# RWKV's triangular inverse by doubling: levels 2 to 4 multiply 32 by 32 blocks, four products of 32 rows for a pair of heads

## The chip, the cores and the metric

One core of a Trainium2 chip runs the whole program. The metric is the device time of one execution in microseconds (us), the median of several executions.

## The reference, cut to what matters

The program computes two transformer-like blocks on 256 tokens of width 1024. The change is inside the second block's bidirectional RWKV-7 mixer (8 heads of 64, two directions):

```python
def _rwkv7_step(state, inp):
    r, w, k, v, kk, kka = inp
    sa = jnp.einsum('dbhvk,dbhk->dbhv', state, kk)
    state = state * w[..., None, :] - sa[..., :, None] * kka[..., None, :] + v[..., :, None] * k[..., None, :]
    y = jnp.einsum('dbhvk,dbhk->dbhv', state, r)
    return state, y
...
_, ys = lax.scan(_rwkv7_step, state0, xs)
```

The kernel does this scan in chunks of 64 tokens. Inside a chunk, `sa` of a token depends on the `sa` of the tokens before it, which is a triangular system of 64 by 64 for each head and direction. The kernel inverts that triangle by doubling: at level n the diagonal blocks of 2^n rows are already inverted, and two products make the inverse of the blocks of 2^(n+1) rows. There are five levels after the first, so that the whole 64 by 64 triangle is inverted after level 5. After level n the inverse is zero outside its diagonal blocks of 2^(n+1) rows, which at levels 1 to 4 are at most 32 rows.

## The kernel before, in words

All matrix products of the linear layers use weights in two parts (high and low). A ring of six weight tiles is filled by SyncE's DMAs (L490), ScalarE makes the high part (L2316), GpSimd the low part (L505), and TensorE multiplies three times (L529 to L531, or L597 to L599 for the products by token). The stage of the change lies between 848 and 945 us of the span, between the projection `qkv` and the output projection `out_2`.

In that stage, 16 cases (8 heads, 2 directions) are worked on for each of four chunks j = 0 to 3. The 16 cases are 8 "units" u of two heads: the first head of a unit is in partitions 0 to 63, the second in partitions 64 to 127. `heads` (L1098 to L1103, the matrix instruction is on L1101) issues two products of 64 by 64 by 64, one for each half of the partitions, and `per_unit` (L1105) calls it for the eight units, so that a call issues 16 products and fills one bank of PSUM, 128 partitions by 512 columns. Operands are f32, and the trace has two matmul records for each such product, so one call of `per_unit` is 32 records ("a product of a level" below means such a call). TensorE loads the left operand as weights and streams the right one past it.

The chunks are worked on in two pairs (two "lanes", j % 2). Per level and chunk the work is:

- `level_left(j, level)` on TensorE (L1147 to L1150): waits for `t_ev`, the transposed inverse of the level before, and multiplies `nt` by `tc` into the lane's bank 1. VectorE's `level_left` masks the result (L2128, called through L2164) into `uc`; the mask of a level is zero outside the blocks that this level joins.
- `level_both(j, level)` on TensorE (L1153 to L1161): waits for `u_ev` (the mask done) and for `tt_ev` (the copy of the level before), and multiplies `uc` by `ttc[j]` into the lane's bank 0. VectorE's `turned` transposes this in 32 by 32 blocks into `tc` (L2169, not after level 5), and ScalarE's `inverse` copies it into `ttc[j]` after that transposition (L2843).

Each engine works off its own list in the order written. For chunks 0 and 1 the TensorE order of a level is

```python
level_left(0, level)
level_left(1, level)
attention(4 + 2 * level)
level_both(0, level)
attention(5 + 2 * level)
level_both(1, level)
```

where `attention` interleaves one head of the dilated attention: an even step is `scores` (L1028) and `weighted_values` (L1048), an odd step is `turned_probabilities` (L1039, which waits for VectorE's L2085 and ScalarE's exponentials L2797). VectorE takes the scores out of PSUM (L2072), reduces them (L2075) and scales the weighted values (L2082, L2085) between its masks and its transpositions.

For chunks 2 and 3 a level is `level_left(2)`, `level_left(3)`, a piece of the chunk recurrence, `level_both(2)`, `level_both(3)`. The pieces are `from_state(0)` at level 1, `solve(0)` at level 2, `to_state(0)` at level 3, `from_state(1)` and `attention_by_feature` (L1075) at level 4 and `solve(1)` at level 5; all but the last-named function use products of 64 rows through `heads`. On VectorE, the norm of the attention (L2100, L2102) stands behind level 1's transpositions, the new state (L2180) and the outputs (L2188) ahead of level 3's transpositions, and the rest of the norm (L2107, L2110) behind them. After level 5, `half_row(0)` starts `out_2` when the last `tt_ev` has come. `first_products`, `second_products` and `third_product`, which make the inputs of the inversion, also use `per_unit`.

Of the kernel before, what the change touches and what calls it, by code (L numbers as in the profile page):

```python
# [44 lines left out]
RC = 64  # L45
# [594 lines left out]
def tensor_program(k, pe):  # L640
    s, mm, c = k.s, k.nc.tensor.matmul, Small(k)
# [29 lines left out]
    for b in range(KB):  # L671
        mm(ps, k.wdt_hi[:, b, :], op.hi[:, b, :], start=b == 0, stop=False)
        mm(ps, k.wdt_hi[:, b, :], op.lo[:, b, :], start=False, stop=False)
        last = mm(ps, k.wdt_lo[:, b, :], op.hi[:, b, :], start=False, stop=b == KB - 1)
# [148 lines left out]
    for i in range(2):  # L823
        for g in range(GROUPS):
            last = mm(k.bank[0][32 * g:32 * g + 32, 0:T], k.ones[:, 0:32], k.gn_sq[:, 2 * g + i, :], start=i == 0, stop=i == 1)
# [272 lines left out]
    def heads(bank, u, lhs, rhs, start=True, stop=True, shared=False):  # L1098

        for rows in (slice(0, HD), slice(HD, P)):  # L1100
            last = mm(bank[rows, u * RC:(u + 1) * RC], lhs[rows], rhs[rows], start=start, stop=stop,  # L1101
                      skip_group_check=shared)
        return last  # L1103

    def per_unit(bank, lhs, rhs):  # L1105

        for u in range(8):
            last = heads(bank, u, lhs(u), rhs(u))
        return last

    C_, B_, A_, Q_ = range(4)
    of = lambda x: lambda u: x[:, u, :]
    stack = lambda u: k.stack[:]
# [27 lines left out]
    def nth(j, level, levels):  # L1141

        return 2 * levels * (j // 2) + 2 * (level - 1) + j % 2 + 1

    def level_left(j, level):

        pe.wait_ge(s["t_ev"], nth(j, level, 5))  # L1147
        if level == 1:
            pe.wait_ge(s["qc_ev"], j + 1)
        per_unit(k.lane[j % 2][1], of(k.nt[j % 2]), of(k.tc[j % 2])).then_inc(s["u_mm"], 1)  # L1150

    def level_both(j, level):

        pe.wait_ge(s["u_ev"], nth(j, level, 5))
        if level == 1:
            pe.wait_ge(s["tt_first"], j + 1)
            pe.wait_ge(s["ac_ev"], j + 1)
            pe.wait_ge(s["bt_ev"], min(j + 1, NRC - 1))
        else:
            pe.wait_ge(s["tt_ev"], nth(j, level - 1, 5))  # L1160
        per_unit(k.lane[j % 2][0], of(k.uc[j % 2]), of(k.ttc[j])).then_inc(s["tt_mm"], 1)  # L1161

    def from_state(j):

# [53 lines left out]
    for level in range(1, 6):  # L1218
# [6 lines that stand above are left out]
# [35 lines left out]
    for level in range(1, 6):  # L1260
        level_left(2, level)
        level_left(3, level)
        if level == 1:
            from_state(0)
        elif level == 2:
            solve(0)
        elif level == 3:
            to_state(0)
        elif level == 4:
            from_state(1)  # L1270
            attention_by_feature()
        else:
            solve(1)
        level_both(2, level)
        level_both(3, level)
# [1666 lines left out]
def build_program(nc, a, out):  # L2942
    with ExitStack() as ctx:
        k = allocate(nc, ctx)
        block = ctx.enter_context(nc.Block())

        @block.sync
        def _(sp):
            sync_program(k, sp, a, out)

        @block.gpsimd
        def _(pool):
            gpsimd_program(k, pool)

        @block.scalar
        def _(act):
            scalar_program(k, act, a)

        @block.vector
        def _(v):  # L2960
            vector_program(k, v)

        @block.tensor
        def _(pe):
            tensor_program(k, pe)
# [84 lines left out]
```

## Time and profile before

| | us |
|---|---|
| median of 3 executions | 1185.81 (1185.35 to 1187.62) |
| the profiled execution, its own time | 1187.46 |
| its span, first to last instruction | 1185.7 |
| TensorE busy | 1154.6 (97%) |
| TensorE weight loads busy | 1079.5 (91%) |
| GpSimd busy | 900.6 (76%) |
| ScalarE busy | 623.7 (53%) |
| VectorE busy | 551.2 (46%) |

Some 1.8 us of the profiled execution lie outside its span. A busy TensorE means that some product is in flight; products overlap in it, so its busy share says that it is rarely empty, and not how full it is.

### The profile page before, as it was taken

How to read it: one execution, taken by the hardware profiler on the slowest of the kernel's cores; microseconds unless marked ns; L12 is line 12 of the kernel's file. 1: busy time of each engine (PE TensorE's matmuls, PEld its weight loads, DVE VectorE, ACT ScalarE, POOL GpSimd, SP SyncE). 2: the span in 40 equal slices, each digit the busy share in tenths (PEclk: the TensorE clock that was granted, in tenths of full speed). 3: DMA queues.
4: the chain of work that ended last, by engine and by line, in shares of the span. 5: the costliest groups of instructions: out<-in, count | busy, mean ns of one | idle time of the engine just before them, and what ended most of it. 6: DMA issues, size and time to landing. Idle time of an engine off the chain costs nothing.

```text
span 1185.7 us, 25232 instructions
## 1 busy us (share of the span) xinstructions
PE 1154.6 (97%) x10632; PEld 1079.5 (91%) x10632; DVE 551.2 (46%) x973; ACT 623.7 (53%) x1001; POOL 900.6 (76%) x689
## 2 busy tenths in 40 slices
PE   6999999999999999999999999999999999999998
PEld 6998999999997899998999999899989988999997
DVE  2553485543662122224644233757876555323334
ACT  5665676447635454444744444689342316444443
POOL 5987677876986999996899998599700015999994
PEclk9999999999999999999999999999999999999999
DMA  7655445655576666665566656556400034666663
GB/s 252 192 180 166 137 125 160 211 158 154 186 218 196 178 190 185 192 183 175 160 187 186 190 184 187 203 161 188 126 3 3 4 109 142 181 191 182 192 181 106
DMA packets 53776, 192.75 MB, mean 163 GB/s; under 512 B 6305, under 2 KB 7329, under 8 KB 53281
## 3 DMA queue, kind: packets, MB, share of 16 engines
q1 hardware_dynamic: 50640, 183.00, 51.1%
q10 hardware_dynamic: 3024, 8.16, 2.0%
q8 instruction: 84, 1.38, 0.5%
q14 instruction: 28, 0.22, 0.1%
HBM read 189.03 MB, written 1.05 MB: 160 GB/s over the span
## 4 chain that ended last, share of the span: by engine, by line
PE 90%; DVE 5%; ACT 2%; DMA 2%; issue 1%; POOL 0%; SPq 0%; DVEq 0%; ACTq 0%
PE product L529 18%; PE product L531 18%; PE product L530 18%; PE bank L597 7%; PE bank L599 7%; PE bank L598 7%; PE bank L1101 3%; PE product L1101 3%; PE product L695 1%; PE product L697 1%; PE product L696 1%; PE product L1048 1%; PE bank L529 1%; PE product L1028 1%; PE bank L530 1%
## 5 line engine op out<-in xcount | busy, mean ns | idle before, releaser
L505 POOL TENSOR_TENSOR weight_lo<-raw_ring,weight_hi 128x512 fp32r<-128x512 f32 x684 | 895.7, 1342 | 267.2 <-ACT weight_hi L2316 246.3
L2316 ACT ACTIVATE weight_hi<-raw_ring 128x1024 fp32r<-128x1024 f32 x338 | 357.0, 1060 | 406.0 <-DMA raw_ring<-in_ffn_gu 107.7
L529 PE MATMUL product<-operand_B_hi,weight_hi 128*128 128x256 f32 x1104 | 311.5, 282 | 1.7 <-POOL weight_lo L505 1.6
L530 PE MATMUL product<-operand_B_lo,weight_hi 128*128 128x256 f32 x1104 | 311.1, 282 | 0.0
L531 PE MATMUL product<-operand_B_hi,weight_lo 128*128 128x256 f32 x1104 | 310.9, 282 | 0.0
L529 PE MATMUL product<-operand_A_hi,weight_hi 128*128 128x256 f32 x776 | 223.7, 288 | 11.3 <-DVE weight_lo L1429 11.3
L531 PE MATMUL product<-operand_A_hi,weight_lo 128*128 128x256 f32 x776 | 219.8, 283 | 0.0
L530 PE MATMUL product<-operand_A_lo,weight_hi 128*128 128x256 f32 x776 | 219.6, 283 | 0.0
L529 PEld LDWEIGHTS product<-operand_B_hi,weight_hi 128*128 128x128 f32 x1104 | 208.0, 188 | 4.9 <-POOL weight_lo L505 2.1
L530 PEld LDWEIGHTS product<-operand_B_lo,weight_hi 128*128 128x128 f32 x1104 | 207.7, 188 | 3.0
L531 PEld LDWEIGHTS product<-operand_B_hi,weight_lo 128*128 128x128 f32 x1104 | 207.8, 188 | 0.0
L529 PEld LDWEIGHTS product<-operand_A_hi,weight_hi 128*128 128x128 f32 x776 | 147.3, 190 | 14.2 <-issue 13.6
L530 PEld LDWEIGHTS product<-operand_A_lo,weight_hi 128*128 128x128 f32 x776 | 146.9, 189 | 0.6 <-issue 0.2
L531 PEld LDWEIGHTS product<-operand_A_hi,weight_lo 128*128 128x128 f32 x776 | 147.0, 189 | 0.0
L597 PE MATMUL bank<-weight_hi,operand_B_hi 128*128 128x512 f32 x304 | 120.1, 395 | 2.5 <-DVE operand_B_lo L1761 2.5
L599 PE MATMUL bank<-weight_lo,operand_B_hi 128*128 128x512 f32 x304 | 119.8, 394 | 0.0
L598 PE MATMUL bank<-weight_hi,operand_B_lo 128*128 128x512 f32 x304 | 119.4, 393 | 0.0
L1761 DVE TENSOR_TENSOR operand_B_lo<-arena,operand_B_hi 128x256 fp32r<-128x256 f32 x76 | 76.3, 1005 | 81.7 <-ACT operand_B_hi L2633 81.7
L1852 DVE TENSOR_TENSOR pre<-product,rs 128x256 f32<-128x256 f32 x84 | 35.1, 418 | 127.3 <-PE product L531 127.3
L1771 DVE TENSOR_TENSOR arena<-product,pre 128x256 f32<-128x256 f32 x30 | 12.7, 425 | 127.7 <-ACT pre L2652 127.7
L597 PEld LDWEIGHTS bank<-weight_hi,operand_B_hi 128*128 128x128 f32 x304 | 57.1, 188 | 13.8 <-issue 2.5
L599 PEld LDWEIGHTS bank<-weight_lo,operand_B_hi 128*128 128x128 f32 x304 | 57.1, 188 | 13.3
(379 smaller groups left out, 1441.0 us busy)
## 6 DMA issues: line engine op xcount, KB each, us to landing
raw_ring<-in_w_in SPq DMA_DIRECT2D x99, 512.0 KB, 3.7
raw_ring<-in_ffn_gu SPq DMA_DIRECT2D x88, 512.0 KB, 3.6
raw_ring<-in_ffn_down SPq DMA_DIRECT2D x44, 512.0 KB, 3.6
raw_ring<-in_w_mlp_up SPq DMA_DIRECT2D x32, 512.0 KB, 4.2
raw_ring<-in_w_mlp_down SPq DMA_DIRECT2D x32, 512.0 KB, 4.2
raw_ring<-in_w_out SPq DMA_DIRECT2D x16, 512.0 KB, 4.2
raw_ring<-in_w_gmlp_v SPq DMA_DIRECT2D x8, 512.0 KB, 4.2
raw_ring<-in_w_branch_c SPq DMA_DIRECT2D x8, 512.0 KB, 3.5
```

What stands on the lines that cost most here:

```text
L505: last = k.nc.gpsimd.tensor_tensor(k.wlo[:, slot, part], k.raw[:, slot, part], k.whi[:, slot, part].bitcast(F32), ALU.subtract)
L529: mm(ps, w_hi, op.hi[:, b, :], start=b == 0, stop=False)
L530: mm(ps, w_hi, op.lo[:, b, :], start=False, stop=False)
L531: return mm(ps, w_lo, op.hi[:, b, :], start=False, stop=b == blocks - 1)
L597: mm(ps, hi, k.whi[:, slot, cols], start=j == 0, stop=False)
L598: mm(ps, lo, k.whi[:, slot, cols], start=False, stop=False)
L599: last = mm(ps, hi, k.wlo[:, slot, cols], start=False, stop=j == n - 1)
L1101: last = mm(bank[rows, u * RC:(u + 1) * RC], lhs[rows], rhs[rows], start=start, stop=stop, skip_group_check=shared)
L1761: nv.tensor_tensor(op.lo[:, j % KB, :], k.hid[:, j % KB, :], op.hi[:, j % KB, :].bitcast(F32), ALU.subtract).then_inc(s["op_ready"], 1)
L1771: nv.tensor_tensor(k.hid[:, j % KB, :], k.product[n][:, 0:T], k.pre[:, j % RING, :], ALU.mult).then_inc(s["evacuated"], 1)
L1852: nv.tensor_tensor(k.pre[:, ring, :], k.product[n][:, 0:T], k.rs[:], ALU.mult).then_inc(s["evacuated"], 1)
L2316: k.nc.scalar.activation(k.whi[:, slot, 0:w], k.raw[:, slot, 0:w], ACT.Copy).then_inc(k.s["hi_ready"], 1)
```

## The change

In levels 2, 3 and 4, `level_left` and `level_both` call a new function in place of `per_unit`. For each of the eight units it issues four products of 32 by 32 by 32 in place of two of 64 by 64 by 64: the two diagonal blocks of each of the two heads. Block q takes rows 32q to 32q + 31 of both operands and writes the same partitions of the bank. What lies outside the diagonal blocks in a bank keeps what the product of level 1 has left there. Levels 1 and 5, and every other user of `per_unit`, stay as they are.

```diff
+    def per_half_unit(bank, lhs, rhs):
+
+        for u in range(8):
+            for q in range(4):
+                rows, cols = slice(32 * q, 32 * q + 32), slice(32 * (q % 2), 32 * (q % 2) + 32)
+                last = mm(bank[rows, u * RC + 32 * (q % 2):u * RC + 32 * (q % 2) + 32], lhs(u)[rows, cols],
+                          rhs(u)[rows, cols], start=True, stop=True)
+        return last
+
+    by_level = lambda level: per_half_unit if 2 <= level <= 4 else per_unit
+
...
     def level_left(j, level):
...
-        per_unit(k.lane[j % 2][1], of(k.nt[j % 2]), of(k.tc[j % 2])).then_inc(s["u_mm"], 1)
+        by_level(level)(k.lane[j % 2][1], of(k.nt[j % 2]), of(k.tc[j % 2])).then_inc(s["u_mm"], 1)
...
     def level_both(j, level):
...
-        per_unit(k.lane[j % 2][0], of(k.uc[j % 2]), of(k.ttc[j])).then_inc(s["tt_mm"], 1)
+        by_level(level)(k.lane[j % 2][0], of(k.uc[j % 2]), of(k.ttc[j])).then_inc(s["tt_mm"], 1)
```

## Rows read from the trace of the kernel before

**Rows 1.** The page: TensorE's line, the granted clock, the chain that ended last.

```profile
PE 1154.6 (97%) x10632; PEld 1079.5 (91%) x10632; DVE 551.2 (46%) x973; ACT 623.7 (53%) x1001; POOL 900.6 (76%) x689
...
PEclk9999999999999999999999999999999999999999
...
PE 90%; DVE 5%; ACT 2%; DMA 2%; issue 1%; POOL 0%; SPq 0%; DVEq 0%; ACTq 0%
```

**Rows 2.** Busy time by stretch: stretch, length, busy and count by engine, clock, DMA.

```profile
873.70:880.50 6.80, 6.80 (x148) 6.02 (x145) 4.56 (x8) 2.78 (x7) 0.00 (x0) 1.00 0.01 2
...
922.10:928.70 6.60, 6.60 (x222) 6.58 (x224) 4.00 (x6) 2.79 (x4) 0.00 (x0) 1.00 0.01 2
```

**Rows 3.** Groups by form, TensorE: weights rows*columns, moving rows x columns, busy, mean ns.

```profile
L1101 PE MATMUL bank<-arena 64*64 64x64 f32 x1280 | 42.3, 220 | 0.9 <-DVE arena L2128 0.9
...
L1048 PE MATMUL product<-arena 128*128 128x64 f32 x64 | 8.8, 281 | 0.8 <-ACT arena L2806 0.8
...
L1007 PE MATMUL bank<-arena,block_ones 128*128 128x256 f32 x8 | 1.9, 379 | 0.0
...
L825 PE MATMUL bank<-arena,ones 128*32 128x256 f32 x16 | 1.1, 385 | 0.0
```

**Rows 4.** Timeline, one level of chunks 0 and 1: start, duration, engine, line.

```profile
866.94 1.10 PE L1101 MATMUL product<-arena 64*64 64x64 f32 x32
...
867.97 1.13 PE L1028 MATMUL product<-arena 64*128 64x256 f32 x4
...
869.03 1.10 PE L1048 MATMUL product<-arena 128*128 128x64 f32 x8
869.14 0.69 DVE L2072 SCALAR_TENSOR_TENSOR arena<-product,arena 128x512 f32<-128x512 f32 x1 [0.36 <-PE product L1028]
...
870.07 1.15 PE L1101 MATMUL bank<-arena 64*64 64x64 f32 x32
...
870.73 0.29 DVE L2085 TENSOR_TENSOR arena<-product,small 128x128 f32<-128x128 f32 x1
...
871.17 0.63 PE L1039 MATMUL product<-ident,arena 128*128 128x128 f32 x4
...
871.73 2.08 PE L1101 MATMUL bank<-arena 64*64 64x64 f32 x64
...
872.93 0.72 DVE L2169 STREAM_TRANSPOSE arena<-bank 128x512 f32<-128x512 f32 x1 [0.95 <-PE bank L1101]
...
873.70 1.15 PE L1101 MATMUL product<-arena 64*64 64x64 f32 x32
```

**Rows 5.** Timeline, levels 2 to 5 of chunks 2 and 3, same columns.

```profile
921.95 0.68 DVE L2128 TENSOR_TENSOR arena<-product,arena 128x512 f32<-128x512 f32 x1
922.09 3.11 PE L1101 MATMUL bank<-arena 64*64 64x64 f32 x96 [0.88 <-DVE arena L2128]
...
924.22 0.72 DVE L2169 STREAM_TRANSPOSE arena<-bank 128x512 f32<-128x512 f32 x1 [0.22 <-PE bank L1101]
...
925.04 3.90 PE L1101 MATMUL product<-arena 64*64 64x64 f32 x128
...
928.77 3.07 PE L1101 MATMUL bank<-arena 64*64 64x64 f32 x96
...
928.99 0.69 DVE L2188 COPY pre<-product 128x512 f32<-128x512 f32 x1 [0.24 <-PE product L1101]
...
931.67 4.83 PE L1101 MATMUL product<-arena 64*64 64x64 f32 x160
...
937.46 3.12 PE L1101 MATMUL bank<-arena 64*64 64x64 f32 x96
940.41 2.03 PE L1101 MATMUL product<-arena 64*64 64x64 f32 x64
```

**Rows 6.** Waits in 840 to 980 us: waiter, releaser, total us, times, longest.

```profile
POOL weight_lo L505 <- ACT weight_hi L2316: 109.8, 4, 84.8
...
PEld bank L1101 <- issue: 2.0, 11, 0.3
```

## The prediction

> **What bounds the kernel now.** I read the page first. TensorE is busy 97% of the span, the chain that ended last is 90% TensorE, and the granted clock is full in every slice [rows 1]. The change touches only the inversion of the triangles, so its stage decides. [...] In a level of chunks 0 and 1 a second chain runs beside TensorE's own and is as long as it: left product of lane 1 (866.94), scores (867.97), VectorE's L2072 (869.14) to L2085 (870.73), turned probabilities (871.17), `level_both(1)` (871.73), its transposition (872.93), next left product of lane 1 (873.70) [rows 4]. The links are 1.03 + 1.17 + 1.59 + 0.44 + 0.56 + 1.20 + 0.77 = 6.76 us. This chain holds only two of the level's four products. In chunks 2 and 3 TensorE waits 0.88 us for VectorE's masks ahead of level 2's `level_both(2)`, and the next left products start right behind VectorE's transpositions: 924.22 + 0.72 = 924.94, then 925.04 [rows 5].
>
> **The size of one product.** 24 calls change (3 levels, 4 chunks, 2 products). One takes 0.93 us: the 128 records from 925.04 to 928.77 are four calls, 3.73 / 4 [rows 5]. That is 16 rounds of 58 ns, each round the two halves of the partitions at once: single records last 220 ns, yet 1280 of them cover 42.3 us, 33 ns each [rows 3].
> What would a round of 32 by 32 cost? Eight records of 256 moving columns cover 1.9 us and one alone is 0.379, so a further one takes (1.9 - 0.379) / 7 = 217 ns, 0.85 ns a column [rows 3]; 64 columns are 54 ns of the 58, and 4 are fixed. Weight columns cost about as much: L1048 streams only 64 columns past 128 weight columns, and its 8 records take 1.10 us, (1.10 - 0.28) / 7 = 117 ns each [rows 3, 4]. With 32 of both I take 27 + 5 = 32 ns a round.
> How many blocks share a round? The new call has 64 records. That four narrow tiles of the array run at once is shown by L825, whose weights are 32 columns wide: 16 records of 256 columns cover 1.1 us, where one after another they would need 15 x 217 + 385 ns = 3.6 us, and four at once 3 x 217 + 385 = 1.04 [rows 3]. There the four differ by columns of the array, here by rows and columns; no row shows four groups of rows, but two groups do overlap. So 64 / 4 = 16 rounds x 32 ns = 0.51 us a call, 0.42 saved. Bounds: 16 x 27 = 0.43 us if nothing is fixed; two at once gives 32 x 32 ns = 1.02; one at a time gives 64 x 32 ns = 2.05. I take 0.51, since both the overlap of halves and the four narrow tiles are in rows.
>
> [...] The bank is one and the same for all four groups of rows, and already now two groups write one bank and run at 58 ns a pair, not 116 [rows 3, 5]. [...]
>
> **Where the saving lies on the path, chunks 0 and 1.** TensorE's own chain has four changed products in a level, 6.80 - 4 x 0.42 = 5.1 us; the other has two, 6.76 - 2 x 0.42 = 5.9 us, and takes over. So only `level_left(1)` and `level_both(1)` count: 2 x 3 levels x 0.42 = 2.5 us. What is late next is VectorE's scores work. The left and both products of chunk 0 cost and give nothing: they lie under L2072 to L2085 and under lane 1's transposition; without that cover they would give another 2.5. Level 5's `level_left(0)` becomes just as late as lane 1's transposition, and it comes right behind a change of tile size. A change of tile size costs 0.10 us from the left product to the scores (866.94 to 867.97 is 1.03, less 0.93) and 0.17 from `level_both(0)` to the transpositions (870.07 to 871.17 is 1.10, less 0.93; a part of it is the wait for L2085) [rows 4]; I take 0.13. One such is on the path: 2.4 us stay.
>
> **Chunks 2 and 3.** Here I follow the lists with the same lags: VectorE starts 0.24 us after a product's last record starts, TensorE 0.06 after VectorE's end, last record 0.48 after the first.
> Level 2: both left products are hidden, as the masks end at 921.95 + 0.68 = 922.63 whatever TensorE does (VectorE is at the attention's norm before them). `level_both(2)` stays at 922.09, `level_both(3)` starts at 922.69 behind its mask, its transposition runs 923.56 to 924.28, and level 3's `level_left(3)` starts at 924.34, not 925.04, and ends 924.85: 1.12 ahead of 925.97.
> Level 3: `to_state(0)` (96 records) is unchanged, less one change of tile size ahead of it and one behind (0.13 each): `level_both(2)` starts at 927.91, not 928.77. VectorE's output copy L2188, 0.69 us, waits for `to_state`'s end and now holds the transpositions back until 928.71; they end at 930.18. Level 4's `level_left(3)` starts at 930.24, not 931.67, and ends 1.85 us ahead.
> Level 4: another 0.13 ahead of `from_state(1)`, so `level_both(2)` is 1.72 us ahead (935.74, not 937.46). The two transpositions end at 937.18 and 937.93, level 5's `level_left(2)` runs 937.24 to 938.17, and `level_left(3)` starts at 938.17, not 940.41. That is 2.24 us ahead, 2.2. Level 5 is unchanged, TensorE works it off without a gap, and `half_row(0)` comes earlier by as much.
>
> **What comes behind.** All of `out_2` and `ffn2` moves up if the weights are there. GpSimd waits 84.8 us in one piece [rows 6] with the ring full, so the first tiles are ready, and the later loads are released by TensorE's own progress: they move with it. I cost this at nothing; if `ffn2` were limited by an absolute time of a DMA, the gain would shrink, but no DMA is in flight in this stage (share 0.01 [rows 2]). The new call has twice the instructions, 128 in place of 64 with the weight loads, on TensorE's list alone; no other engine's list, wait or DMA changes.
>
> Sum: 2.4 + 2.2 = 4.6 us. The profiled execution (span 1185.7, time 1187.46) would take 1182.9; it lies 1.65 above the median of the runs, 1185.81, and against that the forecast is **1181.2 us**. About 0.2%, 2.4 us, is what a measurement of this kernel can tell from no change.
>
> **Rivals.**
> *Two at once (slower).* The four groups of rows do not all overlap, only pairs. For it: nothing in the trace shows four groups of rows. Against: L825's four tiles. A call takes 1.02 us, 0.09 more. TensorE's chain then decides in chunks 0 and 1: 12 x 0.09 + 2 x 0.13 = 1.35 us. In chunks 2 and 3, level 2's left products hide in the 0.88 us gap: 10 x 0.09 + 5 x 0.13 = 1.55. Sum 2.9, **1188.7 us**. The point from which it turns slower is a call of about 0.86 us (54 ns a round of four), where what is saved on the path no longer pays for the changes of tile size. Chance 0.10.
> *One at a time (much slower).* [...] Against it are the pairs in [rows 5]. A call takes 2.05 us, 1.12 more: 12 x 1.12 + 0.3 in chunks 0 and 1, 12 x 1.12 - 0.9 + 0.7 in the others, 27 us, **1213 us**. Chance 0.05. [...]
> *Issue shows up.* A call of 0.93 us hides how TensorE's sequencer takes waits and instructions; one of 0.51 with twice the instructions hides less. The weight loads of L1101 waited for issue 11 times, 2.0 us, 0.18 each [rows 6]. If each changed call on the path (6 and some 8) lost that, 14 x 0.18 = 2.5 us, the gain is 2.1: **1183.7 us**. Against it: most of these waits are at changes of tile size, already counted. Chance 0.15.
> *It does not do what it says.* If all of it were hidden by VectorE, the time would stay at 1185.8; the rows give no cover for lane 1. Chance 0.02.
>
> [...]
>
> **How the numbers follow.** The forecast has a chance of 0.68. Its own range is from 0.43 us a call and free changes of size (6 x 0.50 = 3.0, and 2.24 x 0.50 / 0.42 + 0.4 = 3.1, sum 6.1, 1179.7 us) to about 1182.6 at 0.65 us a call (0.28 / 0.42 x 4.6 = 3.1). The range that should hold 8 in 10 takes in the issue rival and no change, and stops short of the two slow rivals: 1179.6 to 1187.0. Faster by over 0.2% (below 1183.4) takes the forecast and a quarter of the issue rival: 0.72. Within 0.2%: the rest of that rival, no change, and part of the pairs: 0.15. Slower (above 1188.2): 0.13.
>
> **What the changed profile would show.** L1101's neighbour, the new line, has 24 x 64 = 1536 records of 32*32 32x32. A group of 64 of them should last about 0.5 to 0.6 us from first to last start; 1.0 means pairs, 2.0 one at a time. The levels 2 to 4 of chunks 0 and 1 should repeat every 5.9 us, TensorE waiting there for VectorE (L2085 or L2169), where it waited for next to nothing. In chunks 2 and 3 the gap ahead of level 2's masks should grow from 0.9 to about 1.7 us. The stretch behind, from level 5's `level_left(3)` to the end, should keep its length (1185.7 - 940.4 = 245.3 us) within a few tenths. A period of 5.9 with a longer stretch behind would mean that the gain is given back to the weights; a lower granted clock in this stage would be a price that I have not counted.

## The result, and the profile after

| | before | after |
|---|---|---|
| median, us | 1186.50 (4 executions, 1185.35 to 1187.62) | 1201.68 (4 executions, 1197.29 to 1205.73) |
| profiled execution: time, span, us | 1187.46, 1185.7 | 1197.29, 1195.5 |
| mean granted clock of its span | 0.997 | 0.989 |

The ratio is 1.0123, 95% interval 1.0092 to 1.0154: slower by 15 us, where 4.6 us less was forecast. The profiled execution is the fastest of the four. Its page, answering to [rows 1], with the queue that carries the instructions:

```profile
span 1195.5 us, 26768 instructions
...
PE 1155.6 (97%) x11400; PEld 1078.5 (90%) x11400; DVE 548.5 (46%) x973; ACT 623.8 (52%) x1001; POOL 900.2 (75%) x689
...
PEclk9999999999999999999999999999989899999999
...
q8 instruction: 90, 1.47, 0.5%
```

There are 768 more matmul records and as many more weight loads, 1536 instructions, and the clock is no longer full in two of the slices. The queue of instructions moved 90 packets, 1.47 MB: 16 KB each. L1116 is the new products' line, and every line behind it stands 11 further down than before (L2096 was L2085, L2139 was L2128, L2180 was L2169). The timeline of TensorE in the changed levels (start, duration, engine, line, count, idle time before):

```profile
874.59 1.16 PE L1116 MATMUL bank<-arena 32*32 32x32 f32 x110
876.65 0.34 PE L1116 MATMUL bank<-arena 32*32 32x32 f32 x17 [0.89 <-issue]
...
881.26 0.99 PE L1116 MATMUL bank<-arena 32*32 32x32 f32 x92
884.11 0.47 PE L1116 MATMUL bank<-arena 32*32 32x32 f32 x35 [1.86 <-issue]
...
885.27 2.07 PE L1028 MATMUL product<-arena 64*128 64x256 f32 x4
...
895.50 1.13 PE L1028 MATMUL product<-arena 64*128 64x256 f32 x4
...
924.78 2.06 PE L1116 MATMUL bank<-arena 32*32 32x32 f32 x128 [1.64 <-issue]
928.35 0.26 PE L1116 MATMUL bank<-arena 32*32 32x32 f32 x1 [1.51 <-issue]
...
929.39 4.45 PE L1101 MATMUL product<-arena 64*64 64x64 f32 x96
...
939.66 5.37 PE L1101 MATMUL product<-arena 64*64 64x64 f32 x128
...
945.98 1.35 PE L1116 MATMUL bank<-arena 32*32 32x32 f32 x128
```

The two calls at 945.98 take 1.35 us, the last record's 0.2 included: about 0.58 us a call, so the four groups of rows do overlap, as forecast. But TensorE stops in the middle of calls, inside one and the same product form, and waits for nothing that the trace shows. Between the stops at 924.78 and 928.35 lie 128 matmul records and, as each has its own load, 256 instructions. And the four `scores` records at 885.27 take 2.07 us, where they took 1.13 in [rows 4]: the clock is halved (0.52 over 885.2 to 895.5). The waits for issue from 840 to 980 us (waiter, releaser, total, times, longest) and the busy time by stretch (length, busy time and count of PE, PEld, DVE, ACT, POOL, then granted clock, DMA share, GB/s) say how much of each:

```profile
PE bank L1116 <- issue: 6.8, 5, 1.9
PE product L1116 <- issue: 2.5, 2, 1.7
```

```profile
869.20:875.60 6.40, 5.92 (x324) 5.00 (x318) 4.64 (x9) 3.10 (x8) 0.00 (x0) 1.00 0.02 5
875.60:882.30 6.70, 5.45 (x269) 4.48 (x259) 4.41 (x9) 2.81 (x8) 0.00 (x0) 1.00 0.02 5
882.30:885.20 2.90, 1.09 (x100) 1.09 (x99) 1.01 (x2) 0.66 (x2) 0.00 (x0) 0.93 0.00 0
885.20:895.50 10.30, 10.30 (x218) 8.76 (x210) 4.71 (x9) 2.77 (x7) 0.00 (x0) 0.52 0.02 5
...
925.00:935.00 10.00, 8.20 (x382) 7.71 (x381) 4.59 (x7) 2.79 (x4) 0.00 (x0) 0.66 0.02 5
935.00:945.00 10.00, 7.36 (x291) 7.01 (x291) 3.66 (x6) 1.79 (x3) 0.00 (x0) 0.83 0.02 5
```

So there are two costs: seven stops for issue, 9.3 us, against none in `before` at this line, and a granted clock of 0.5 for most of 885 to 895 us and parts of 925 to 935 and of 935 to 945. By the trace's clock record these are 884.8 to 895.1, 925.8 to 932.6 and 939.4 to 942.8, 20.5 us in all. The first row also shows 642 instructions in 6.40 us without a stop: 10.0 ns each, so for two or three blocks TensorE went faster than it did for long (14.6 ns each in the burst below).

Since the work ahead of the stage varies by some us from one execution to the next, I compare the stage by itself: from the start of level 1's first transposition (L2169 in `before`) to the first L597 of `out_2` (first the two lines of `before`, then those of the change):

```profile
871.26 0.72 DVE L2169 STREAM_TRANSPOSE arena<-bank 128x512 f32<-128x512 f32 x1 [0.24 <-PE bank L1101]
...
945.01 0.50 PE L597 MATMUL bank<-weight_hi,operand_A_hi 128*128 128x512 f32 x1 [0.70 <-ACT arena L2843]
```

```profile
867.72 0.72 DVE L2180 STREAM_TRANSPOSE arena<-bank 128x512 f32<-128x512 f32 x1 [0.24 <-PE bank L1101]
...
953.28 0.50 PE L597 MATMUL bank<-weight_hi,operand_A_hi 128*128 128x512 f32 x1 [0.70 <-ACT arena L2854]
```

It took 945.01 - 871.26 = 73.7 us before and 953.28 - 867.72 = 85.6 us after, 11.8 more. Behind it the span is 240.7 us before and 242.2 after.

### The profile page after: what moved, and what is told of

It is laid out like the page before. It is cut to its first block, busy times and chain, and to the rows that moved or that the text cites. A ratio compares the mean times of both kernels' runs of the same rounds, so it can differ in the third digit from the quotient of the medians.

```text
span 1195.5 us, 26768 instructions
## 1 busy us (share of the span) xinstructions
PE 1155.6 (97%) x11400; PEld 1078.5 (90%) x11400; DVE 548.5 (46%) x973; ACT 623.8 (52%) x1001; POOL 900.2 (75%) x689
## 3 DMA queue, kind: packets, MB, share of 16 engines
q8 instruction: 90, 1.47, 0.5%
## 4 chain that ended last, share of the span: by engine, by line
PE 90%; DVE 4%; ACT 2%; DMA 2%; issue 2%; POOL 0%; DVEq 0%; ACTq 0%
PE product L529 18%; PE product L530 18%; PE product L531 18%; PE bank L597 7%; PE bank L599 7%; PE bank L598 7%; PE product L1101 3%; PE bank L1101 2%; PE product L1028 1%; PE bank L1116 1%; DMA raw_ring<-in_w_in 1%; PE product L695 1%; PE product L697 1%; PE product L696 1%; PE bank L529 1%
## 5 line engine op out<-in xcount | busy, mean ns | idle before, releaser
L597 PE MATMUL bank<-weight_hi,operand_B_hi 128*128 128x512 f32 x304 | 120.1, 395 | 2.5 <-DVE operand_B_lo L1772 2.5
L1772 DVE TENSOR_TENSOR operand_B_lo<-arena,operand_B_hi 128x256 fp32r<-128x256 f32 x76 | 79.3, 1044 | 87.3 <-ACT operand_B_hi L2644 87.3
L597 PEld LDWEIGHTS bank<-weight_hi,operand_B_hi 128*128 128x128 f32 x304 | 57.2, 188 | 13.7 <-issue 2.5
```

Source lines behind the costliest of these rows:

```text
L597: mm(ps, hi, k.whi[:, slot, cols], start=j == 0, stop=False)
L1772: nv.tensor_tensor(op.lo[:, j % KB, :], k.hid[:, j % KB, :], op.hi[:, j % KB, :].bitcast(F32), ALU.subtract).then_inc(s["op_ready"], 1)
```

## The experiments

The first theory (F) is that TensorE runs out of instructions; the rivals are that the 32-row form or its change of tile size stops TensorE, whatever the count (T), and a clock that the 32-row form itself lowers (C). Later C2 joins them: the clock falls because TensorE stands still for a part of the time. Ratios are against `before` on the same chip. Stage, issue waits and the time at clock 0.5 inside the stage are those of the one profiled execution. The last column is the median over the executions of the mean granted clock of a span (`before`, on the chips of the experiments: 0.997 to 0.999).

| run | ratio, 95% interval | stage, us | issue waits in it, us | clock 0.5 in it, us | clock |
|---|---|---|---|---|---|
| before | 1 | 73.7 | 0 | 0 | 0.997 |
| the change | 1.0123, 1.0092 to 1.0154 | 85.6 | 9.3 | 20.5 | 0.988 |
| chunk 1 alone | 0.9983, 0.9971 to 0.9994 | 72.0 | 0 | 0 | 0.998 |
| the same again | 0.9988, 0.9976 to 1.0 | 71.8 | 0 | 0 | 0.998 |
| half blocks | 1.0013, 1.0 to 1.0027 | 75.0 | 0 | 17.1 | 0.988 |
| burst | one execution, 1217.34 us | 104.9 | 14.7 | 27.3 | 0.986 |
| chunks 0 and 1 | 1.0023, 1.0005 to 1.0041 | 75.4 | 2.0 | 6.8 | 0.994 |
| chunks 2 and 3 | 1.007, 1.0046 to 1.0094 | 83.1 | 8.2 | 10.2 | 0.993 |
| 64-row twice | 1.021, 1.0176 to 1.0244 | 94.5 | 0 | 0 | 0.996 |
| chunk 0 alone | 1.0002, 0.9985 to 1.0019 | 73.7 | 0 | 0 | 0.997 |
| chunks 1 and 3 | 1.0019, 1.0003 to 1.0036 | 75.2 | 2.3 | 0 | 0.997 |
| half blocks in 1 and 3 | 0.9977, 0.9958 to 0.9996 | 71.1 | 0 | 0 | 0.998 |
| half blocks, filled | 1.0032, 1.0012 to 1.0051 | 72.3 | below 0.2 | 3.4 | 0.993 |
| half the units | 0.9953, 0.9935 to 0.9971 | 68.0 | 0 | 0 | 0.998 |

### A burst of the new form

```diff
     def level_both(j, level):
...
+        if (j, level) == (3, 4):
+            for n in range(16):
+                per_half_unit(k.lane[1][0], of(k.uc[1]), of(k.ttc[3]))
         per_unit(k.lane[j % 2][0], of(k.uc[j % 2]), of(k.ttc[j])).then_inc(s["tt_mm"], 1)
```

> The kernel before with level 4's second product of chunk 3 preceded by 16 calls of the 32-row form (same operands, same bank), 2048 instructions more in one stretch without any change of tile size or any wait. F: the stretch takes about 2048 / 256 x 3.5 = 28 us, with a gap after each 256 instructions, and the clock is halved in it. T: the stretch takes 16 x 0.55 = 9 us with no gap inside, as nothing changes size there. C: 16 x 0.55 us at full clock, 18 us if the clock is halved, no gaps.

The timeline of TensorE in the burst, and two of its stretches, then the queues' packets from 938.1 to 964.3 us (GB/s in 40 slices):

```profile
938.03 1.29 PE L1116 MATMUL bank<-arena 32*32 32x32 f32 x128 [1.13 <-issue]
941.77 1.68 PE L1116 MATMUL bank<-arena 32*32 32x32 f32 x128 [2.46 <-issue]
945.79 1.93 PE L1116 MATMUL bank<-arena 32*32 32x32 f32 x128 [2.34 <-issue]
...
964.25 0.42 PE L1116 MATMUL bank<-arena 32*32 32x32 f32 x12 [1.82 <-issue]
```

```profile
938.00:941.70 3.70, 1.29 (x128) 1.18 (x128) 0.00 (x0) 0.00 (x0) 0.00 (x0) 1.00 0.02 4
...
949.50:953.50 4.00, 1.93 (x128) 1.79 (x128) 0.00 (x0) 0.00 (x0) 0.00 (x0) 0.50 0.01 4
```

```profile
GB/s 0 0 25 0 0 0 0 0 25 0 0 0 0 0 25 0 0 0 0 25 0 0 0 0 0 25 0 0 0 0 25 0 0 0 0 25 0 0 0 0
...
q8 instruction: 7, 0.11, 1.6%
```

This is the disputed cost by itself. Nothing changes size here, nothing waits for another engine, and TensorE still stops after each 128 records and 128 loads. From 938.03 to 964.25 seven blocks of 256 instructions go by in 26.2 us, 3.75 us each, of which the work is 1.1 us at full clock ((1.29 - 0.19), the last record's own time left out). The pace is about the same with the clock full (3.74, the first) and halved (3.47 to 4.02), so it is not TensorE's array that sets it. All 16 calls took 28.9 us (935.71 to 964.60): F gave 28, T 9, and C 18 without gaps. T falls, and C alone does.

The instruction queue moves one packet of 16 KB a block: seven in this stretch for seven blocks. The packets' own records show that each takes 0.9 to 1.1 us and ends 1.2 to 1.6 us before TensorE starts again, at either clock (the first one in the view starts at 939.47, and TensorE starts at 941.77). So the stops keep step with the arrival of instructions. The blocks of 256 of theory F agree with the trace, and in this stream of small matmuls their arrival is not hidden: of the 3.75 us of a block, 1.5 to 2.5 are a wait for issue.

### The same count of instructions in the old form

```diff
+    def twice(bank, lhs, rhs):
+        per_unit(bank, lhs, rhs)
+        return per_unit(bank, lhs, rhs)
+
+    by_level = lambda level: twice if 2 <= level <= 4 else per_unit
```

> The kernel before with each of the 24 calls of levels 2 to 4 issued twice in the 64-row form: as many instructions as in the changed kernel, at 14.6 ns each. F: no issue wait over 0.5 us, full clock, since the blocks arrive about as fast as they are used (3.5 us against 3.7); time up by the work alone, 24 x 0.93 less the slack = 21 us, 1207. If the number of instructions in itself cost something (another wait for each, a pause per block), the time is above that, with gaps.

Its stage took 94.5 us, 20.8 more for 21 expected. The median of its two executions, 1211.31 us, is 24.1 above the kernel before on that chip; some 3 us of this lie outside the stage, and no run explains them. These are all of TensorE's waits from 866 to 970 us (L2858 is L2843 of before, L2100 is L2085):

```profile
PE bank L597 <- ACT arena L2858: 0.7, 1, 0.7
PE product L1039 <- DVE arena L2100: 0.2, 1, 0.2
```

As many instructions as in the change, and no wait for issue: 256 of them last 3.7 us in this form (14.6 ns each), which is the pace of the blocks in the burst (3.75 us). The number brought no wait by itself; it is the number per time.

### Only some of the chunks

The condition `2 <= level <= 4` gets an addition: `and j == 1`, `and j < 2`, `and j >= 2`, `and j == 0`, `and j % 2`.

> Only chunk 1's six calls (levels 2 to 4) use the 32-row products. Theory F (TensorE's instructions arrive in blocks of 256, one block in some 3.5 us at best, and the stalls are TensorE running out of them): a level of chunks 0 and 1 then holds about 430 instructions, 5.9 us at that pace, just what VectorE's chain allows. No issue wait over 0.5 us, full clock, period 5.9 us, time about 2.4 us below before: 1184. Rival T (it is the 32-row tile form, or the change between tile sizes, that stalls TensorE, whatever the count): with more changes of size per product than in the full change, stalls of 1 to 2 us as in the changed kernel and a time above before, about 1189. Rival C (the halved clock comes from 32-row products themselves): clock halved in this stage, no gain.

> The run on chunk 1 alone once more, for its ratio and for a second trace: 0.9975 to 0.999 of before, levels of chunks 0 and 1 of 6.0 to 6.3 us, full clock in them, no issue wait over 0.5 us.

The second trace of chunk 1 alone, one level:

```profile
875.88 1.15 PE L1101 MATMUL bank<-arena 64*64 64x64 f32 x32
876.98 0.64 PE L1039 MATMUL product<-ident,arena 128*128 128x128 f32 x4
877.54 0.75 PE L1116 MATMUL bank<-arena 32*32 32x32 f32 x64
878.23 1.15 PE L1101 MATMUL bank<-arena 64*64 64x64 f32 x32
879.31 0.75 PE L1116 MATMUL product<-arena 32*32 32x32 f32 x64
879.99 1.13 PE L1028 MATMUL product<-arena 64*128 64x256 f32 x4
...
882.08 1.15 PE L1101 MATMUL bank<-arena 64*64 64x64 f32 x32
```

A level takes 882.08 - 875.88 = 6.20 us, not 6.80, without any wait for issue. TensorE's own chain binds: a call with its change of size takes 0.68 (879.31 to 879.99), not 0.51. The level was expected at 5.9 us in the first of the two runs. With six calls this gains 1.8 and 1.9 us in the stage, 2.4 expected. It is the one version here that computes everything and came out below both kernels, by 0.12 and 0.17%; the upper end of the second interval is 1.0, so the gain is at the edge of what can be told.

> The 32-row form in all twelve calls of chunks 0 and 1, chunks 2 and 3 as before. A level of chunks 0 and 1 has about 560 instructions. F: 7.6 us a level at the fetch pace in place of 6.8, so some 2 to 4 us lost there with stalls of 1 to 2 us, and another few if the clock is halved; nothing lost in chunks 2 and 3: 1188 to 1191 us. T: about half of the full change's loss, 1194.

> The 32-row form in all twelve calls of chunks 2 and 3, chunks 0 and 1 as before. F: this stretch ran at about 450 instructions in 6.6 us before, which is already near the pace of one block of 256 in 3.5 us; with 12 x 64 more, three blocks, it loses about 3 x 3.5 = 10 us less what the calls save and less slack: 5 to 9 us over before, 1192 to 1196 us, most of the full change's loss. T: about half of it, as in the run on chunks 0 and 1.

The waits for issue, first of chunks 0 and 1, then of chunks 2 and 3:

```profile
PE bank L1101 <- issue: 1.1, 1, 1.1
PE bank L1116 <- issue: 0.9, 1, 0.9
```

```profile
PE bank L1116 <- issue: 4.4, 3, 2.1
PE product L1116 <- issue: 3.0, 2, 2.0
PE product L1101 <- issue: 0.8, 1, 0.8
```

Twelve calls each, and 2.0 against 8.2 us of stops, a loss of 0.2% against 0.7%. Some of each loss is the clock, which stood at 0.5 for 6.8 and 10.2 us of the stage. F said so from the counts: chunks 2 and 3 had 222 + 224 instructions in 6.60 us before [rows 2], 3.8 us a block, and no room for more; a level of chunks 0 and 1 had 148 + 145 in 6.80. T does not tell them apart.

> Only chunk 0's six calls use the 32-row form: as many calls as in the run on chunk 1 alone. By the chain of waits of the prediction nothing is on the path here: levels stay at 6.8 us, no issue wait over 0.5 us, the time is that of before, 0.999 to 1.002 of it. TensorE gets short idle pieces instead (some 0.8 us a level). Theory C2 (the clock falls after stretches in which TensorE is idle for a tenth of the time, whether for instructions or for VectorE, and not because of the 32-row form): the clock may fall here, and a level that it hits takes 8 us or more. If the clock depended on the form alone, this run and the one on chunk 1 would be alike (full clock).

Every level took 6.8 us, the stage 73.7, the ratio is 1.0002: the six calls of chunk 0 are hidden, as the prediction's second chain had it. The clock stayed full, though TensorE was busy only 6.32 us of 6.80:

```profile
871.80:878.60 6.80, 6.32 (x209) 5.36 (x208) 4.43 (x9) 2.78 (x7) 0.00 (x0) 1.00 0.01 2
```

> The 32-row form in chunks 1 and 3 (twelve calls). F: chunks 0 and 1 as in the run on chunk 1 alone, about 1.8 us gained. In chunks 2 and 3, 384 instructions more are one and a half blocks, 5 us at 3.6 us a block, against some 2 us saved and little slack: 2 to 4 us lost, with one or two issue waits of 1 us. Sum 0 to 2 us above before, 1187 to 1189. If the stalls did not come from the instructions, chunk 3 would gain another 1 to 2 us like chunk 1: 1183.

Chunks 0 and 1 gained 2.0 us (second to eighth transposition 18.45 us, before 20.41). Chunks 2 and 3 lost 3.0 from their first to their last transposition (25.2 for 22.2) and 0.3 behind it, with 2.3 us of waits for issue. This is what F expected of the stage; the whole came out at 1189.16 us, just above its 1187 to 1189.

### Half of the work, to take the instructions away

```diff
-            for q in range(4):
+            for q in (0, 2):
```

> The changed kernel with only blocks q = 0 and 2 of each unit: half of the inverse of levels 2 to 4 is left out. All 24 calls use the 32-row form, with 64 instructions a call as before the change. F: hardly any issue wait, clock full, 1181 to 1184 us. T and C: stalls and halved clock as in the changed kernel, 1195 us or more.

Here half of the inverse of levels 2 to 4 is left out. F alone was wrong, and so was its time: 1188.88 us, for 1181 to 1184. No stop for issue is left, as F said and T did not, but the clock is halved all the same (timeline and stretch):

```profile
886.61 2.07 PE L1028 MATMUL product<-arena 64*128 64x256 f32 x4
```

```profile
881.90:895.60 13.70, 13.47 (x244) 11.46 (x239) 6.55 (x14) 5.57 (x14) 0.00 (x0) 0.50 0.01 2
```

Ahead of the fall TensorE was busy 5.30 of 5.90 us. Was it the idle time, then, or the form? Three runs were made for that.

> As the run before, but with blocks q = 0 and 2 alone in chunks 1 and 3 (half of the inverse of their levels 2 to 4 is left out), so no more instructions than before the change, and chunks 0 and 2 in the 64-row form that keeps TensorE busy. C2: clock full in chunks 0 and 1 (it was halved for 13.7 us with half blocks in all chunks), levels of 5.9 to 6.2 us there, and with no block of instructions added a further 1 to 2 us gained in chunks 2 and 3: 1182.5 to 1184. If the 32-row form with half of the array unused lowers the clock, it falls here too and the gain is gone.

("The run before" is the one on chunks 1 and 3.) Full clock, the stage 2.6 us shorter than before, of which chunks 0 and 1 give 2.3. The time is 1184.5 us, for 1182.5 to 1184. With the form in every second chunk alone the clock stays.

The next run adds to the half blocks one 64-row product of chunk 0 a level (`if j == 0 and 2 <= level <= 4: per_unit(...)` ahead of `level_left`).

> The half-block run (q = 0 and 2 in all chunks, half of the inverse of levels 2 to 4 left out), and ahead of chunk 0's first product of levels 2 to 4 the 64-row product once more, into the same bank: 0.93 us of extra work a level, laid where TensorE was idle. C2 (the clock fell because TensorE stood still for a tenth of the time): TensorE is busy 98% or more of these levels, the clock stays full, levels take about 6.2 us, and first to eighth transposition 18.5 to 19 us, where the half-block run without the extra work took 21.4: more work, less time. If the form lowers the clock, it is halved here as well and the levels take 7 us or more.

This one settles nothing. The profiled execution had the full clock in the levels of chunks 0 and 1 and shorter ones than without the extra work (19.9 us against 21.4 from second to eighth transposition). But TensorE was busy only 6.09 of 6.50 us, not 98%, the clock was halved for 3.4 us in chunks 2 and 3, and in the other executions it was 0.989 to 0.994.

```profile
875.50:882.00 6.50, 6.09 (x182) 5.24 (x177) 4.29 (x9) 2.77 (x7) 0.00 (x0) 1.00 0.02 5
```

So the idle time was given to the old form:

```diff
+    def half_the_units(bank, lhs, rhs):
+        for u in range(4):
+            last = heads(bank, u, lhs(u), rhs(u))
+        return last
+
+    by_level = lambda level: half_the_units if 2 <= level <= 4 else per_unit
```

> The kernel before with only units 0 to 3 in the 24 calls of levels 2 to 4 (half of the inverse of those levels is left out): 64-row form, 0.47 us a call and half the instructions, so TensorE stands still about as much as with half blocks in all chunks, without the 32-row form and without more instructions. If standing still is enough to lower the clock, mean clock 0.988 to 0.993 over the executions, halved for 7 to 14 us somewhere in these levels, time near before. If it is the 32-row form (fewer rows of the array at work in each product), the clock stays at 0.997, levels of chunks 0 and 1 take 5.9 us, and the time is 4 to 5 us below before.

Here, too, half of the inverse of those levels is left out. L2185 is L2169 of before.

```profile
877.95 0.68 PE L1101 MATMUL product<-arena 64*64 64x64 f32 x16 [0.35 <-DVE arena L2185]
878.56 1.13 PE L1028 MATMUL product<-arena 64*128 64x256 f32 x4
...
883.81 0.68 PE L1101 MATMUL product<-arena 64*64 64x64 f32 x16 [0.35 <-DVE arena L2185]
```

```profile
877.00:883.00 6.00, 5.23 (x93) 4.29 (x88) 4.34 (x8) 2.91 (x9) 0.00 (x0) 1.00 0.01 3
```

TensorE is busy 5.23 of 6.00 us, less than with half blocks, at clock 1.00; the six executions had 0.996 to 1.0. The time is 0.9953 of before, the stage 5.7 us shorter. So standing still alone is not what halves the clock here, nor is the number of instructions, which half blocks left as before. What the runs with a halved clock in the stage have in common, against all others, is 32-row products in both lanes (or the burst); that is a pattern over fourteen traces, and what in the form does it was not tested. Single falls of 3.4 us stand outside the stage too, where nothing was changed (861.5 to 864.9 in the second run of chunk 1 alone). With stage lengths of 68.0 and 75.0 us, the two runs with half of the work differ by 7.0 us, for some 17 us at clock 0.5 in the latter's profile; a part of the 7.0 is changes of tile size, which only the latter has more of.

## Why the prediction was wrong

**The size of one product** held roughly: 0.55 us in the burst, 0.58 in the change, for 0.51. The four groups of rows write one bank at 9 ns a record (0.58 us for 64). Both slow rivals of the prediction (pairs at 1.02 us a call, one at a time at 2.05) fell.

**Where the saving lies** held well. With half the units, which gives short calls (0.47 us) without new changes of size, more instructions or a lower clock, the levels of chunks 0 and 1 took 5.86 us (883.81 - 877.95) for 5.9. TensorE waited there for L2185 and L2101, which are L2169 and L2085 of before, as named. The stage gained 5.7 us; the prediction's own sum for such calls, 6 x 0.46 + 2.24 x 0.46 / 0.42 + 0.4, gives 5.6. Chunk 0's calls alone were worth nothing, as written. One thing was left out: the changes of size on TensorE's own chain. With chunk 1 alone two calls a level change, and 6.80 - 2 x 0.42 + 2 x 0.13 = 6.2 is the level that was measured, not 5.9.

**The step that failed** is the sentence "The new call has twice the instructions, 128 in place of 64 with the weight loads, on TensorE's list alone", costed at nothing. The rival *issue shows up* named the place and mis-sized the term: it took 0.18 us a call, 2.5 us on the path, from waits at changes of size. The waits for issue were 9.3 us, and they come by the block of 256, not by the call. The price stood in rows that were read: 222 + 224 instructions in 6.60 us [rows 2] is 14.8 ns each, and no stretch of that trace went faster for long. I took that for the array's time and not for a bound, so that the upper end for 128 instructions, 128 x 14.8 ns = 1.9 us a call, was missing from the bounds of the product. It belonged there. The twelve calls of chunks 2 and 3 took 16.9 us of TensorE's list with their waits, 1.4 us each, which is nearer to 1.9 than to 0.51.

**The second miss** is the clock. The prediction named it in its last sentence and gave it no chance. Its share in the change: the stage is 16.4 us longer than forecast (+11.8 for -4.6), 9.3 of it are the waits for issue, and 7.1 are left for some 20 us at half clock. Rows give nearly as much. From the scores of level 4 to those of level 5 the change took 10.2 us (885.27 to 895.50), while the run on chunks 0 and 1 took 7.9 for the same calls, 1.1 of it a stop for issue:

```profile
886.17 1.23 PE L1028 MATMUL product<-arena 64*128 64x256 f32 x4
...
894.07 1.13 PE L1028 MATMUL product<-arena 64*128 64x256 f32 x4
```

That is 3.4 us. The 96 and 128 old products behind took 4.45 and 5.37 us, for 3.07 and 3.90 in [rows 5], 2.9 more. So 6.3 us of the 7.1 are found; the split is still worked out from single traces. The executions of the change spread over 8.4 us, and the two ends agree with their clocks (1205.73 at 0.986, 1197.29 at 0.989).

**What stays open:** why a block takes 3.4 to 4.0 us when the DMA engines are all but idle (share 0.02 in the burst). Its packet takes 0.9 to 1.1 us of it; the rest are two lags, 1.0 to 1.7 us from TensorE's start to the next packet and 1.2 to 1.6 from that packet's end to TensorE's next start, and no run says what they are made of. Open as well is what in the stretches with 32-row products brings the granted clock down to 0.5.

## What to carry to other kernels

Before you cut matmuls into more and smaller ones, count the instructions per microsecond of that stretch, weight loads included, and compare them with the fastest pace that the trace sustains: here 256 in 3.75 us, 14.6 ns each. Where the old form already ran at that pace, as here in chunks 2 and 3 (14.8 ns each), smaller products only turned work into waiting (8.2 us of waits for issue, 0.7% slower). Calls of half the length with half the instructions were worth 5.7 us in the stage, where calls of nearly half the length with twice the instructions cost 11.8. Apply such a form only to the calls on the critical chain: six calls of 24 kept a gain of 0.12 and 0.17%, at the edge of what can be told.

## What had not been expected of the hardware

TensorE's instruction stream has a ceiling of its own, one block of 256 in 3.75 us on average over seven blocks, at either clock (1.00 and 0.50) and with the DMA engines all but idle (share 0.01 to 0.02), though in the change 642 instructions went by in 6.40 us before the first stop. Stretches with 32-row products in both lanes, and the burst, were granted a clock of 0.5 for 3 to 27 us at a time (after TensorE had been busy 5.30 of 5.90 us, with half blocks), whereas about the same idle time with 64-row products (busy 5.23 of 6.00 us, half the units) left the clock at 1.00.
